# Hybrid streaming encoder step: token-quarter sums in two sets of temporaries, and seven more seven-product pairs in the up projections

## What is computed

```python
def swiglu_ffn(x, w_in, w_out):
    g, u = jnp.split(x @ w_in, 2, axis=-1)
    return (jax.nn.silu(g) * u) @ w_out

xp = xp + swiglu_ffn(rmsnorm(xp, ffn_norms[i]), *ffn_params[i])
y_prompt = rmsnorm(xp, final_norm)
```

## Time and profile before

| | |
|---|---|
| median of 3 runs | 2585.49 us (2583.73 to 2587.84) |
| the profiled execution | 2584.34 us |
| its span | 2582.6 us |
| TensorE matmul busy | 2549.6 us (99%), 20065 matmuls |
| VectorE busy | 1688.8 us (65%) |
| ScalarE busy | 1179.4 us (46%) |
| granted TensorE clock, mean | 0.997 |

### The profile page before, as it was taken

One profiled execution on the slowest core, in us unless ns is written; L12 is line 12 of the kernel. 1 busy time (PEld: TensorE's weight loads), 2 busy tenths in 40 slices (PEclk: granted clock), 3 DMA queues, 4 the chain that ended last, 5 costly groups with the idle time before them and its releaser, 6 DMA issues.

```text
span 2582.6 us, 48134 instructions
## 1 busy us (share of the span) xinstructions
PE 2549.6 (99%) x20065; PEld 2483.3 (96%) x20065; DVE 1688.8 (65%) x2465; ACT 1179.4 (46%) x1778; POOL 171.9 (7%) x182
## 2 busy tenths in 40 slices
PE   8999999999999999999999999999999999999998
PEld 8999999999988899999998899999999999999998
DVE  5555793884555579479557556947955555884872
ACT  5454551543555555245345644524524553541443
POOL 2101000001000010000112210000011101000001
PEclk9999999999999999999999999999999999999999
DMA  4222333332433233333222222333322223333322
GB/s 117 70 76 82 99 93 96 99 95 73 124 99 104 77 92 96 91 102 93 84 69 80 72 86 76 97 98 93 100 81 79 72 73 90 98 92 96 94 84 80
DMA packets 441634, 230.68 MB, mean 89 GB/s; under 512 B 16884, under 2 KB 437968, under 8 KB 441440
## 3 DMA queue, kind: packets, MB, share of 16 engines
q1 hardware_dynamic: 439792, 226.89, 30.7%
q10 hardware_dynamic: 1200, 0.59, 0.1%
q0 software_dynamic: 448, 0.45, 0.1%
HBM read 219.03 MB, written 8.87 MB: 88 GB/s over the span
## 4 chain that ended last, share of the span: by engine, by line
PE 95%; DVE 3%; issue 1%; ACT 1%; DMA 0%; DVEq 0%; ACTq 0%
PE slot L2255 53%; PE aux L2734 14%; PE slot L2734 14%; PE aux L2255 4%; PE aux L2223 2%; PE aux L2636 1%; PE aux L2400 1%; PE aux L2642 1%; PE aux L2548 1%; PE aux L2486 1%; DVE w_lo L1397 1%; PE aux L2415 1%; PE aux L2418 0%; PE slot L2695 0%; PE aux L2290 0%
## 5 line engine op out<-in xcount | busy, mean ns | idle before, releaser
L734 ACT ACTIVATE w_hi<-raw 128x1024 fp32r<-128x1024 f32 (+5 forms) x231 | 265.3, 1148 | 346.9 <-PE slot L2255 315.0
L2255 PE MATMUL slot<-xg_hi,w_hi 128*128 128x272 f32 x1856 | 401.8, 298 | 12.5 <-DVE w_lo L1397 10.0
L2255 PE MATMUL slot<-xg_hi,w_lo 128*128 128x272 f32 x1856 | 383.8, 288 | 0.0
L2255 PE MATMUL slot<-xg_lo,w_hi 128*128 128x272 f32 x1856 | 383.7, 288 | 0.0
L1397 DVE TENSOR_TENSOR w_lo<-raw,w_hi 128x1024 fp32r<-128x1024 f32 (+4 forms) x229 | 309.7, 1352 | 69.3 <-ACT w_hi L734 68.6
L2255 PEld LDWEIGHTS slot<-xg_hi,w_hi 128*128 128x128 f32 x1856 | 291.1, 189 | 25.1 <-DVE w_lo L1397 12.4
L2255 PEld LDWEIGHTS slot<-xg_lo,w_hi 128*128 128x128 f32 x1856 | 291.9, 189 | 0.0
L2255 PEld LDWEIGHTS slot<-xg_hi,w_lo 128*128 128x128 f32 x1856 | 290.8, 189 | 0.0
L2255 PE MATMUL slot<-h_hi,w_hi 128*128 128x272 f32 x1386 | 286.1, 288 | 0.7 <-issue 0.7
L2255 PE MATMUL slot<-h_hi,w_lo 128*128 128x272 f32 x1386 | 285.9, 287 | 0.0
L2255 PE MATMUL slot<-h_lo,w_hi 128*128 128x272 f32 x1386 | 285.6, 287 | 0.0
(11 more groups left out here) (391 smaller groups left out, 5859.3 us busy)
## 6 DMA issues: line engine op xcount, KB each, us to landing
raw<-in_l_ffn_w_out_dram SPq DMA_DIRECT2D x64, 704.0 KB, 4.6
raw<-in_l_ffn_w_in_dram SPq DMA_DIRECT2D x72, 512.0 KB, 4.6
raw<-in_l_gla_w_in_dram SPq DMA_DIRECT2D x48, 512.0 KB, 3.8
ffn_raw_b<-in_l_ffn_w_in_dram SPq DMA_DIRECT2D x70, 256.0 KB, 3.5
ffn_raw_b<-in_l_ffn_w_in_dram SPq DMA_DIRECT2D x35, 512.0 KB, 5.2
raw<-in_l_ffn_w_in_dram SPq DMA_DIRECT2D x68, 256.0 KB, 3.3
raw<-in_l_att_w_qkv_dram SPq DMA_DIRECT2D x24, 512.0 KB, 3.8
raw<-in_l_lru_w_in_dram SPq DMA_DIRECT2D x24, 512.0 KB, 3.8
```

Of the source, the lines that this page charges most:

```text
L734: act.activation(w_hi[par][:, 0:kt, :], raw[par][:, 0:kt, :], ACT.Copy).then_inc(s_hi, 1)
L2255: ins = pe.matmul((slot[par] if bank is None else bank)[:, hf, 0:HALF], w[par][:, k, :], a[:, k0 + k, hf * HALF:(hf + 1) * HALF], start=(k ...
```

## The change

It does four things. (1) Two sets of `xq` and `tq`: in the first pair's window both parts 0 and 1 are scaled and summed (the sums before rstd is copied), and their `t_low` comes behind the next weights; parts 2 and 3 follow in the second window. `t_low` is cut into `t_sum` and `t_low`. (2) `UP_PAIRS[1]` begins with S; so up1's first S pair has its sums made in the last block of down0. (3) `LAST_PAIRS` is all S. (4) u of layer 3's up1 is no longer multiplied by rstd; `last_project` scales its result by rstd instead and then adds.

```diff
--- before.py
+++ after.py
-UP_PAIRS = ("CCCSSSSSSSS", "CSSSSSSSSSS")
-LAST_PAIRS = "CSSCSSCSSCS"
-T_PART = {0: (0,), 1: (1, 2), 2: (3,)}
+UP_PAIRS = ("CCCSSSSSSSS", "SSSSSSSSSSS")
+LAST_PAIRS = "SSSSSSSSSSS"
+T_X_AT, T_HI_AT = (1, 2, 5, 6), (3, 4, 7, 8)
+T_SUM_AT, T_LO_AT = (0, 3, 8, 11), (7, 8, 15, 16)
...
-                h_count[i, hf, u] = max(h_count.values(), default=0) + (kind == "S") + scaled
+                h_count[i, hf, u] = max(h_count.values(), default=0) + (kind == "S")
...
-                sb("ffn_front0", [P, FH - 2, TOK], F32, c)
-                xq = sb("ffn_xq", [P, 4, HALF], F32, c)
-                sb("ffn_front1", [P, FH - 2, TOK], F32, c)
-                tq = sb("ffn_tq", [P, 4, HALF], F32, c)
+                sb("ffn_front0", [P, FH - 4, TOK], F32, c)
+                xq = [sb(f"ffn_xq{n}", [P, 4, HALF], F32, c) for n in range(2)]
+                sb("ffn_front1", [P, FH - 4, TOK], F32, c)
+                tq = [sb(f"ffn_tq{n}", [P, 4, HALF], F32, c) for n in range(2)]
...
+            if name == "down0" and up_kinds(i, 1, layers)[0] == "S":
+                return "seven"
...
-                    act.wait_ge(s_free, b0 + m + 1)
+                    act.wait_ge(s_xd, XT * (2 * i + 1) + m + 1)
...
+                        if j and nxt == "seven":
+                            hi_sums((i, 1, 0), b0 + XT, None)
+                            hi_more_sums((i, 1, 0), b0 + XT, None)
+                        else:
+                            split(b0 + m2 * 2 + (j + 1), (p0 + j + 1) % 2, nxt if j else kt)
...
+            def t_x(i, q):
+
+                norm, xq = f"l{i}_norm_ffn", FF["xq"][q % 2]
+                if q >= 2:
+                    act.wait_ge(s_tdve, 16 * i + T_SUM_AT[q - 2] + 3)
+                elif i:
+                    act.wait_ge(s_tdve, 16 * i)
+                act.activation(xq[:, 0:2, :].rearrange("p a n -> p (a n)"), one(x, q), ACT.Copy, scale=gain(norm, q))
+                act.activation(xq[:, 2:4, :].rearrange("p a n -> p (a n)"), one(x, q + KQ), ACT.Copy,
+                               scale=gain(norm, q + KQ)).then_inc(s_tact, 1)
+
             def t_high(i, q):
 
-                n, norm = KQ * i + q, f"l{i}_norm_ffn"
-                if n:
-                    act.wait_ge(s_tdve, 4 * n)
-                act.activation(FF["xq"][:, 0:2, :].rearrange("p a n -> p (a n)"), one(x, q), ACT.Copy, scale=gain(norm, q))
-                act.activation(FF["xq"][:, 2:4, :].rearrange("p a n -> p (a n)"), one(x, q + KQ), ACT.Copy,
-                               scale=gain(norm, q + KQ)).then_inc(s_tact, 1)
-                act.wait_ge(s_tdve, 4 * n + 3)
-                act.activation(one4(FF["t_hi"], q), FF["tq"][:, :, :], ACT.Copy).then_inc(s_tact, 1)
+                act.wait_ge(s_tdve, 16 * i + T_SUM_AT[q] + 3)
+                act.activation(one4(FF["t_hi"], q), FF["tq"][q % 2][:, :, :], ACT.Copy).then_inc(s_tact, 1)
...
                 if hf == 0 and u == 0:
                     stat(stat_of[i, "ffn"])
+                    t_x(i, 0)
+                    t_x(i, 1)
...
-                for q in T_PART.get(u, ()) if hf == 0 else ():
-                    t_high(i, q)
+                if hf == 0 and u == 1:
+                    t_x(i, 2)
+                    t_x(i, 3)
+                    t_high(i, 2)
...
+                if hf == 0 and u < 2:
+                    t_high(i, (0, 3)[u])
+                if hf == 0 and u == 0:
+                    t_high(i, 1)
...
-                    dve.tensor_tensor(halves(one(x, m)), slot[(b0 + m) % 2][:, :, 0:HALF], halves(one(x, m)),
-                                      ALU.add).then_inc(s_free, 1)
+                    if m:
+                        dve.wait_ge(s_xd, XT * (2 * i + 1) + m)
+                    dve.tensor_tensor(FF["y"][:, 0:2, :], slot[(b0 + m) % 2][:, :, 0:HALF], halves(rstd[:, :]),
+                                      ALU.mult).then_inc(s_free, 1)
+                    dve.wait_ge(s_free, b0 + m + 1)
+                    dve.tensor_tensor(one(x, m), FF["g"], one(x, m), ALU.add).then_inc(s_xd, 1)
                 m = XT - 1
                 for c, (cols, tiles) in enumerate(END_PARTS):
                     dve.wait_ge(s_eh, c + 1)
-                    dve.tensor_tensor(one(x, m, cols), slot[(b0 + m) % 2][:, c, 0:cols.stop - cols.start], one(x, m, cols),
-                                      ALU.add).then_inc(s_ea, 1)
+                    dve.tensor_tensor(FF["u"][:, cols], slot[(b0 + m) % 2][:, c, 0:cols.stop - cols.start], rstd[:, cols],
+                                      ALU.mult).then_inc(s_free, 1)
+                    dve.wait_ge(s_free, b0 + m + 1 + c)
+                    dve.tensor_tensor(one(x, m, cols), FF["u"][:, cols], one(x, m, cols), ALU.add).then_inc(s_ea, 1)
...
+                        if j and nxt == "seven":
+                            w_sums((i, 1, 0), b0 + XT)
+                            lo_sums((i, 1, 0), b0 + XT)
+                            lo_more_sums((i, 1, 0), b0 + XT, 2)
+                        else:
+                            split(b + 1, (p0 + j + 1) % 2, nxt if j else kt)
...
-                if (i, hf) == (last, 1):
-                    if kinds[u] == "S":
-                        dve.wait_ge(s_h, h_no[at] - 1)
-                    else:
-                        dve.wait_ge(s_free, b + 2)
-                    dve.tensor_tensor(FF["u"], FF["u"], rstd[:, :], ALU.mult).then_inc(s_h, 1)
...
+            def t_sum(i, q):
+
+                at, xq, tq = 16 * i + T_SUM_AT[q], FF["xq"][q % 2], FF["tq"][q % 2]
+                dve.wait_ge(s_tact, 8 * i + T_X_AT[q])
+                if q >= 2:
+                    dve.wait_ge(s_tdve, 16 * i + T_LO_AT[q - 2])
+                elif i:
+                    dve.wait_ge(s_tdve, 16 * i)
                 dve.tensor_tensor(tq[:, 0:2, :], xq[:, 0:4:3, :], xq[:, 1:2, :].broadcast_to([P, 2, HALF]),
                                   ALU.subtract).then_inc(s_tdve, 1)
-                dve.wait_ge(s_tdve, 4 * n + 1)
+                dve.wait_ge(s_tdve, at + 1)
                 dve.scalar_tensor_tensor(tq[:, 2, :], xq[:, 3, :], -1.0, tq[:, 0, :], ALU.mult, ALU.subtract).then_inc(s_tdve, 1)
-                dve.wait_ge(s_tdve, 4 * n + 2)
+                dve.wait_ge(s_tdve, at + 2)
                 dve.scalar_tensor_tensor(tq[:, 3, :], tq[:, 2, :], -1.0, xq[:, 2, :], ALU.mult, ALU.subtract).then_inc(s_tdve, 1)
-                dve.wait_ge(s_tact, 2 * n + 2)
-                dve.tensor_tensor(one4(FF["t_lo"], q), tq[:, :, :], one4(FF["t_hi"], q).bitcast(F32),
+
+            def t_low(i, q):
+
+                dve.wait_ge(s_tact, 8 * i + T_HI_AT[q])
+                dve.tensor_tensor(one4(FF["t_lo"], q), FF["tq"][q % 2][:, :, :], one4(FF["t_hi"], q).bitcast(F32),
                                   ALU.subtract).then_inc(s_tdve, 1)
...
-                    stat(stat_of[i, "ffn"], rstd)
+                    stat_inv(stat_of[i, "ffn"])
+                    t_sum(i, 0)
+                    t_sum(i, 1)
+                    stat_take(stat_of[i, "ffn"], rstd)
...
-                for q in T_PART.get(u, ()) if hf == 0 else ():
-                    t_low(i, q)
+                if hf == 0 and u == 1:
+                    t_sum(i, 2)
+                    t_sum(i, 3)
+                    t_low(i, 2)
...
+                if hf == 0 and u == 0:
+                    t_low(i, 0)
+                    t_low(i, 1)
+                if hf == 0 and u == 1:
+                    t_low(i, 3)
...
-                a11_second = up_kinds(i, hf, layers)[u - 1] == "S"
+                a11_second = u > 0 and up_kinds(i, hf, layers)[u - 1] == "S"
...
-                pe.wait_ge(s_tdve, 4 * KQ * (i + 1))
+                pe.wait_ge(s_tdve, 16 * (i + 1))
```

More of the change, by code:

```diff
@@ L168, in up_plan @@
         for hf in range(2):
-            run, scaled = 0, (i, hf) == (layers - 1, 1)
+            run = 0
             for u, kind in enumerate(up_kinds(i, hf, layers)):
-                h_count[i, hf, u] = max(h_count.values(), default=0) + (kind == "S") + scaled
+                h_count[i, hf, u] = max(h_count.values(), default=0) + (kind == "S")
                 run = run + 1 if kind == "S" else 0
@@ L1196, in two @@
                     for j in range(2):
-                        split(b0 + m2 * 2 + (j + 1), (p0 + j + 1) % 2, nxt if j else kt)
+                        if j and nxt == "seven":
[3 more added lines that the diff above has]
+                            split(b0 + m2 * 2 + (j + 1), (p0 + j + 1) % 2, nxt if j else kt)
                         if norm:
@@ L1281, in h_high @@
             def h_high(i, hf, u, kinds):
-                if kinds[u] == "S" or (i, hf) == (last, 1):
+                if kinds[u] == "S":
                     act.wait_ge(s_h, h_no[i, hf, u])
@@ L1310, in up_window @@
                 if now == "S":
-                    if prev == "C":
+                    if prev != "S":
                         hi_a11(at, b, prev)
@@ L1990, in two @@
```

(22 more changed lines are left out.)

## The result

The changed kernel takes 2556.59 us (median of 4 runs, 2554.18 to 2557.35) against 2584.94 for the kernel before beside it: ratio 0.9887, 95% interval 0.987 to 0.9904, 28 us faster. The profiled execution took 2556.29 us, span 2554.5. The forecast was 2554.2 with a range of 2551.5 to 2561.

What follows compares the result with a forecast made beforehand. TensorE, busy 99% of the span, was taken as the bound. Pairs -10.4, gaps -21.9 and tail +0.96 sum to -31.3 us: 2584.34 becomes 2553.0, plus 1.15 to the median gives 2554.2 us, range 2551.5 to 2561.

Steps and rivals of the forecast that it cites:

- Steps 1 to 3: Up1: seven C pairs become S pairs, 10.4 us less; new first S pair ready 1.7 us early; steady S pairs cost 0.
- Steps 4 and 5: Up0: TensorE's gaps before the second and third C pairs close, weights' low parts early by 0.5 and 0.8 us.
- Step 6: Up0, all four layers: closing both gaps saves 21.9 us, including slow clock and first matmuls after each gap; bounds 0 and 21.9.
- Step 7: Tail, last_project: the extra scaling by rstd stands on the path twice in the last block, +0.96 us; bounds 0.46 to 1.5.
- The rival of slow clock elsewhere: Remaining TensorE waits in mixers and at stage starts catch up to three slow stretches of 1.52 us: up to 2558.8; 8%.
- The other rivals: Weights' low part still late, 16%; both gaps stay whole, 5%; VectorE bounds up1's S pairs, 3%; pairs keep kind, under 1%.

Runs made afterwards that it cites:

- the pairs alone: The changed kernel with the old token sums (one set of temporaries, old order): 2574.79 us against 2585.18 for the kernel before.
- the sums alone: The changed kernel with the old tables of pair kinds (UP_PAIRS and LAST_PAIRS as before): 2567.61 us against 2585.18 for the kernel before.

## Why the prediction was right, and where its size was off

**Steps 1 to 3 (seven pairs, the new first S pair, steady S pairs) held.** 84 matmuls fewer, 1.48 us a pair; the pairs alone gave 10.4 us where I had 9.5 with the tail, well inside that measurement's interval. The preparation was ready 1.8 us early (I had 1.7), S pairs stayed at 10.55 us with VectorE busy 10.36. The slack is as small as I said: one more multiplication of 0.72 us made VectorE the bound.

**Steps 4 and 5 (both gaps close) held in every layer**, with 0.8 us in hand at the first where I had 0.5, and 1.5 at the second where I had 0.8.

**Step 6 is a size read off one execution.** "I take 21.9" is right for the trace it was read from: against that trace the gaps, pairs and tail came out within 0.3 us. But two of its slow stretches, 1.52 us each, are in the kernel before only in some executions, and what its gaps always cost is four times 4.7, 18.9 us. The four traces of kernels with these gaps have 21.9 twice and 18.8 twice. And the same trace has the earliest start of the twelve, 297.6; the two with cheap gaps start at 302.2 and 301.6 once the gaps are off. Its dear gaps and its early start cancelled, so that its total lay close to the median; the change takes away the first and not the second. By that the forecast of the median came out too low; what share each of the two has in the missing 2.4 us no run tells.

With 18.9 the sum is -10.4 - 18.9 + 0.9 = -28.4 us, with 21.9 it is -31.4. Measured side by side three times, the two kernels differ by 28.3, 27.6 and 30.5 us, and the interval of the first is 25 to 34 us. So the medians alone do not tell the two apart; all executions together (12 of the changed kernel, 32 of the one before) differ by 28.7 us. The same correction brings the sums alone from 21.0 to 18.0, measured 17.6.

**Step 7 (the tail) held**: 0.96 forecast, about 0.9 by the stretches behind layer 3's first S pair once the pairs are taken off. The first of its two waits is 0.22 us, not 0.4.

**The rival of slow clock elsewhere**, given 8%, described the profiled execution: two slow stretches in the first 35 us. But the kernel before has them too, so they are no consequence of the shift. The other rivals did not come. Of the Trainium skill's rule (TensorE: Matmul & The Clock Gate, Part 1), that the window of the clock's monitor runs free of the program, the traces agree with what I set aside in the sum: the same kernel, with the same gaps, had slow stretches behind the first gap (layer 0), the second (layers 2 and 3) or neither (layer 1). What I had not seen is that the place decides the price.

## What to carry over

A wait that has a second wait behind it can hide a slow stretch; so price a gap by the least that several executions show, and count what a slow clock adds as a range, not as a term. A total near the median does not make an execution typical in its parts: take several before reading a term off. Where one engine's order decides, look for its idle time ahead of the critical instruction and move work there: here that alone was worth 1.5 us a layer. And before a faster scheme is used throughout, check the second busiest engine within its period: with 0.2 us of slack in 10.55, a multiplication of 0.72 us more turned 4.45 us gained into nothing.

## Not expected of the hardware

Idle stretches of TensorE of 1.9 to 2.3 us were followed by a granted clock of about 0.5 (1.2 GHz) in some executions of the same program and by 1.00 in others. After the two gaps of up0 it came once in 13 of 16 layers, in four traces, and never twice. After a wait of 3.33 us it came in three layers of four; those first S pairs took 1.8 to 2.8 us longer, where a slow stretch behind the gaps of 2 us cost 1.5. After the four waits of 1.25 us it came in none.
